# Reordering the opening of the expert layer in a two-layer decoder step

## The reference, cut to what matters

```python
scores = sigmoid(x @ w_router)                      # 264 x 64
biased = scores + router_bias
# 4 of 8 groups by the sum of their 2 best experts, then 8 of the experts left
idx    = top_k(where(group_open, biased, -inf), 8)
w      = scores[idx] / sum(scores[idx]) * 2.5
routed = sum over the 8 experts e of w[e] * (silu(x @ w_gate[e]) * (x @ w_up[e])) @ w_down[e]
shared = (silu(x @ ws_gate) * (x @ ws_up)) @ ws_down
f      = routed + shared
```

## Time and profile before

| what | us |
|---|---|
| runs, median of 3 (lowest, highest) | 1641.63 (1640.94, 1641.82) |
| span of the profiled execution | 1639.0 |
| TensorE busy in it | 1542.3 (94%) |
| VectorE / ScalarE / GpSimd busy | 734.1 / 372.5 / 96.3 |
| mean granted TensorE clock | 0.990 of full speed |
| first instruction of the opening, layer 0 (logits) | 369.33 |
| first product of round 0, layer 0 / layer 1 | 406.84 / 1122.11 |

### The profile page before, as it was taken

How to read it: one execution, slowest core, us unless ns; L and a number is a source line. 1 busy time by engine, 2 the same in 40 slices (tenths; PEclk the granted TensorE clock), 3 DMA queues, 4 the chain that set the end, 5 groups by cost and what they waited for, 6 DMA issues and landing times. The chain is left out here.

```text
span 1639.0 us, 29881 instructions
## 1 busy us (share of the span) xinstructions
PE 1542.3 (94%) x11300; PEld 1034.8 (63%) x11300; DVE 734.1 (45%) x2034; ACT 372.5 (23%) x784; POOL 96.3 (6%) x121
## 2 busy tenths in 40 slices
PE   6999989998999999999999899998999999999996
PEld 4778765776655655665565587766565566566553
DVE  3205435226464445345345335354745434533445
ACT  2002443113121121122111245332112112111122
POOL 0000100001000000000000001010000000000000
PEclk9999999999999999999999999999999999999998
DMA  9996799337999999999899783986999999998994
GB/s 366 386 371 245 291 397 388 110 129 323 376 420 420 420 420 420 419 419 418 344 390 416 245 267 122 375 320 259 419 420 421 420 420 421 418 418 342 378 420 187
DMA packets 150665, 580.21 MB, mean 354 GB/s; under 512 B 17341, under 2 KB 62561, under 8 KB 101290
## 3 DMA queue, kind: packets, MB, share of 16 engines
q1 hardware_dynamic: 134442, 535.74, 82.4%
q0 software_dynamic: 15488, 40.92, 6.5%
q10 hardware_dynamic: 640, 2.26, 0.3%
HBM read 568.22 MB, written 26.90 MB: 363 GB/s over the span
## 5 line engine op out<-in xcount | busy, mean ns | idle before, releaser
L2391 PE MATMUL ps<-ring,scratch 128*64 128x256 f32 x3840 | 428.5, 383 | 17.7 <-DMA ring<-in_moe_w_up 16.4
L2391 PEld LDWEIGHTS ps<-ring,scratch 128*64 128x64 f32 x3840 | 289.7, 138 | 143.6 <-issue 26.9
L2439 PE MATMUL ps<-ring,scratch 128*64 128x512 f32 x960 | 214.7, 597 | 0.2 <-DVE scratch L2837 0.2
L2352 PE MATMUL ps<-scratch 128*128 128x264 bf16 x1488 | 183.1, 277 | 5.2 <-issue 4.3
L2776 DVE SCALAR_TENSOR_TENSOR scratch<-scratch,ps 128x256 f32<-128x256 f32 x64 | 30.8, 481 | 348.5 <-ACT scratch L2929 341.6
L697 PE MATMUL ps<-hT,ring 128*128 128x264 f32 x768 | 180.5, 389 | 1.3 <-ACT hT L379 1.3
L2352 PEld LDWEIGHTS ps<-scratch 128*128 128x128 bf16 x1488 | 131.3, 97 | 57.8 <-issue 19.6
L697 PEld LDWEIGHTS ps<-hT,ring 128*128 128x128 f32 x768 | 146.0, 192 | 30.7 <-issue 2.5
L2439 PEld LDWEIGHTS ps<-ring,scratch 128*64 128x64 f32 x960 | 62.4, 136 | 126.2 <-issue 93.3
L2743 DVE TENSOR_TENSOR scratch<-scratch,ps 128x264 f32<-128x264 f32 x240 | 103.4, 431 | 76.7 <-PE ps L2352 76.4
L2929 ACT ACTIVATE scratch<-ps 128x256 f32<-128x256 f32 x64 | 24.6, 385 | 441.2 <-PE ps L2391 421.5
(11 more groups left out here) (403 smaller groups left out, 1376.2 us busy)
## 6 DMA issues: line engine op xcount, KB each, us to landing
ring<-in_moe_w_gate SPq DMA_DIRECT2D x128, 1024.0 KB, 17.6
ring<-in_moe_w_up SPq DMA_DIRECT2D x128, 1024.0 KB, 17.6
ring<-in_moe_w_down SPq DMA_DIRECT2D x128, 1024.0 KB, 18.2
ring<-in_ada_w SPq DMA_DIRECT2D x48, 1024.0 KB, 13.7
ring<-in_ret_w_in SPq DMA_DIRECT2D x24, 1024.0 KB, 16.9
ring<-in_state_ret SPq DMA_DIRECT2D x16, 1024.0 KB, 14.6
out_ret_sample<-ring POOLq DMA_DIRECT2D x16, 1024.0 KB, 9.1
ring<-in_gla_w_in SPq DMA_DIRECT2D x12, 1024.0 KB, 13.3
```

What stands on the lines that cost most here:

```text
L2352: mm = nc.tensor.matmul(k.ps[:, c % 2, 0:T], parts_of(p)[:, s, c * P:(c + 1) * P], slot_token[:, p, :], start=(p == 0 and s == 0), stop=(p ...
L2391: mm = nc.tensor.matmul(k.ps[lo:lo + CAP, 2 + p, j * DE:(j + 1) * DE], xg[:, p, c, lo:lo + CAP], slot(k, n, DE)[:, c, :], start=(c == 0), ...
L2439: mm = nc.tensor.matmul(k.ps[lo:lo + CAP, 6 + half, :], hid_t[:, p, m, lo:lo + CAP], slot(k, n, D)[:, m, half * 512:(half + 1) * 512], sta ...
```

## The change

Both expert layers are built by the same code, so the change holds twice. Its parts:

- TensorE transposes the scores ahead of token piece 0. Piece 1 gets PSUM banks 4 and 5 (`TOKEN_BANK`) and no longer waits; piece 2 waits for the copy of piece 0 and stands two chunks into the first half of the shared gate product. ScalarE copies and stores all three pieces before its first Silu.
- The ranks are placed 2 chunks into the second block of shared gate products, the row list of round 0 four chunks later.
- The gather of tile 0 stands ahead of the shared down product, the gather of tile 1 behind its first two chunks, then `slots_first`, then the other six chunks. The wait for both gathers' landing (`s_got`, 32) is therefore ahead of the shared down product.
- The row list of round 1 moves from ahead of round 0 to behind the gate and up products of its tile 0.
- VectorE turns the row list into indices ahead of the first two weight operations. `list_order` is split: its first part (`find_special`, to L2601) runs ahead of the shared hidden product, its second part after the copies of the gathered tiles.
- ScalarE copies its half of tile 0 ahead of the shared down chunks, its half of tile 1 behind the second chunk.

```diff
+    TOKEN_BANK = (6, 4, 6)
...
+        def gather_tile(pe, p, d):
+            for b in range(2):
+                if p:
+                    pe.wait_ge(g_odd if b else g_even, d + p)
+                for c in range(4):
+                    d0 = (4 * b + c) * P
+                    mm = nc.tensor.transpose(k.ps[:, b, c * P:(c + 1) * P], xtok_of(p)[:, d0:d0 + P], ident)
+                mm.then_inc(s_gat, 1)
...
+                if first and p == 0:
+                    list_rows(pe, 1)
...
+            if first:
+                pe.wait_ge(s_shx, DC)
             for p in range(min(tiles(r), PAIRS)):
                 hidden_first(pe, p, 6 + p, d)
...
+            def shared_down(chunks):
+                w = slot(k, n_sh + 2, D)
+                for c in chunks:
+                    if c >= 4:
+                        pe.wait_ge(s_shx, c - 3)
+                    for m in range(FC):
+                        mm = nc.tensor.matmul(k.ps[:, DOWN_BANK[c % 4], 0:T], w[:, m, c * P:(c + 1) * P], sh_hid[:, m],
+                                              start=(m == 0), stop=(m == FC - 1))
+                    mm.then_inc(s_shd if c < DC - 1 else k.ring_free[(n_sh + 2) % RING], 1)
...
-            token_major(0, *TOKENS[0])
             pe.wait_ge(s_frow, 1)
             cond_transpose(k, k.ps[:, 2], fill_rows).then_inc(s_fcrt, 1)
             pe.wait_ge(s_sig, 1)
...
-            token_major(1, *TOKENS[1])
+            token_major(0, *TOKENS[0], bank=TOKEN_BANK[0])
+            token_major(1, *TOKENS[1], bank=TOKEN_BANK[1])
             wait_slot(k, pe, n_sh)
             pe.wait_ge(s_fmod, 1)
-            shared(0, 0, range(DC)).then_inc(s_shg, 1)
-            token_major(2, *TOKENS[2])
-            shared(0, 1, range(DC)).then_inc(k.ring_free[n_sh % RING], 1)
+            shared(0, 0, range(2))
+            pe.wait_ge(s_natc, 1)
+            token_major(2, *TOKENS[2], bank=TOKEN_BANK[2])
+            shared(0, 0, range(2, DC)).then_inc(s_shg, 1)
+            shared(0, 1, range(2))
             pe.wait_ge(s_ch, 1)
...
+            shared(0, 1, range(2, 6))
+            pe.wait_ge(s_natc, TT)
+            list_rows(pe, 0, bank=6)
+            shared(0, 1, range(6, DC)).then_inc(k.ring_free[n_sh % RING], 1)
             wait_slot(k, pe, n_sh + 1)
             shared(1, 0, range(DC))
-            pe.wait_ge(s_natc, TT)
-            list_rows(pe, 0, bank=6)
             shared(1, 1, range(DC)).then_inc(k.ring_free[(n_sh + 1) % RING], 1)
+            pe.wait_ge(s_idxc, 1)
+            pe.wait_ge(s_got, 16 * PAIRS)
+            gather_tile(pe, 0, 0)
+            wait_slot(k, pe, n_sh + 2)
+            pe.wait_ge(s_shh, FC)
+            shared_down(range(2))
+            gather_tile(pe, 1, 0)
             pe.wait_ge(s_eye, 1 + 3 * (PAIRS + 1))
             pe.wait_ge(s_w0, 1)
-            pe.wait_ge(s_shh, FC)
             slots_first(pe)
-            ...
-            gather(pe, 0)
-            pe.wait_ge(s_shx, DC)
-            list_rows(pe, 1, bank=6)
+            shared_down(range(2, DC))
+            pe.wait_ge(s_shx, DC - 2)
             pe_round(pe, 0)
...
-            link(nc.vector.tensor_tensor(weight, score, chosen, ALU.mult))
-            link(nc.vector.tensor_reduce(total, weight, AX.X, ALU.add))
             v.wait_ge(s_idx, 1)
             row_numbers(PAIRS, bank=6, to=first_rows_at).then_inc(s_idxc, 1)
+            link(nc.vector.tensor_tensor(weight, score, chosen, ALU.mult))
+            link(nc.vector.tensor_reduce(total, weight, AX.X, ALU.add))
...
                 "p t (b e) s -> p b t (e s)", b=PAIRS)).then_inc(s_w0, 1)
+            find_special(v)
             wait_used(k, v, n_sh + 1)
...
+            take(v, 0, 0, nc.vector.tensor_copy, g_even)
             list_order(v)
             next_slots(1, [expert_at(v, EPI + e) for e in range(EPI)])
-            take(v, 0, 0, nc.vector.tensor_copy, g_even)
...
             token_rows_out(0, P)
             token_rows_out(1, P)
+            token_rows_out(2, NS)
             for m in range(FC):
...
-                if m == 0:
-                    token_rows_out(2, NS)
...
+            take_tile(act, 0, 1, nc.scalar.copy, g_odd, 0)
             for c in range(DC):
...
+                if c == 1:
+                    take_tile(act, 1, 1, nc.scalar.copy, g_odd, 0)
-            take(act, 0, 1, nc.scalar.copy, g_odd)
```

More of the change, by code:

```diff
@@ L2287, in gather @@
                 mm.then_inc(s_gat, 1)
+        def gather(pe, r, late=0):
+            d = done_tiles(r, late)
+            pe.wait_ge(s_got, 16 * (d + tiles(r)))
+            for p in range(tiles(r)):
+                gather_tile(pe, p, d)
         def spread_slots(pe, p):
@@ L2462, in _, with token_major @@
         def _(pe):
-            def token_major(t, n0, n):
-                if t:
-                    pe.wait_ge(s_natc, t)
+            def token_major(t, n0, n, bank):
                 for c in range(DC):
-                    mm = nc.tensor.transpose(k.ps[0:n, 6 + c // 4, (c % 4) * P:(c % 4 + 1) * P],
+                    mm = nc.tensor.transpose(k.ps[0:n, bank + c // 4, (c % 4) * P:(c % 4 + 1) * P],
                                              k.h[:, c, n0:n0 + n], ident)
@@ L2562, in weights_of, with take_tile @@
             return nc.vector.tensor_copy(to, w_parts[:, :, bass.ds(e, 1), :].rearrange("p t o s -> p t (o s)"))
+        def take_tile(eng, p, b, copy, sem, d):
+            eng.wait_ge(s_gat, 2 * d + 2 * p + b + 1)
+            copy(xg_of(p)[:, 4 * b:4 * b + 4, :].rearrange("p c n -> p (c n)"), k.ps[:, b, :]).then_inc(sem, 1)
         def take(eng, r, b, copy, sem, late=0):
             for p in range(tiles(r)):
-                eng.wait_ge(s_gat, 2 * done_tiles(r, late) + 2 * p + b + 1)
-                copy(xg_of(p)[:, 4 * b:4 * b + 4, :].rearrange("p c n -> p (c n)"), k.ps[:, b, :]).then_inc(sem, 1)
+                take_tile(eng, p, b, copy, sem, done_tiles(r, late))
         def last_of(kind, r, p):
@@ L2583, in rows_done, with find_special @@
                 eng.wait_ge(k.ring_free[n % RING], r + n // RING + 1)
-        def list_order(v):
+        def find_special(v):
             link = lambda ins: k.dve.link(v, ins)
@@ L2601, in list_order @@
             link(nc.vector.tensor_reduce(taken[0:1, 0:7], same, AX.X, ALU.add))
+        def list_order(v):
+            link = lambda ins: k.dve.link(v, ins)
             link(nc.vector.tensor_scalar(ordered[0:1, 0:7], taken[0:1, 0:7], -1.0, None, ALU.mult))
@@ L2851, in _ @@
             v.sem_inc(s_add, DC)
+            take(v, 0, 0, nc.vector.tensor_copy, g_even)
             list_order(v)
             next_slots(1, [expert_at(v, EPI + e) for e in range(EPI)])
[L2854 removed]
             v.wait_ge(s_idx, 2)
[L2856 removed]
+            row_numbers(PAIRS).then_inc(s_idxc, 1)
             round_(0)
@@ L2874, in token_rows_out @@
                 act.wait_ge(s_nat, t + 1)
+                bank = TOKEN_BANK[t]
                 nc.scalar.copy(token_rows[0:n, t, :].rearrange("p (k q) -> p k q", k=DC),
-                               k.ps[0:n, 6:8, :].rearrange("p b (q k) -> p k (b q)", k=DC)).then_inc(s_natc, 1)
+                               k.ps[0:n, bank:bank + 2, :].rearrange("p b (q k) -> p k (b q)", k=DC))\
+                    .then_inc(s_natc, 1)
                 act.wait_ge(s_natc, t + 1)
```

5 lines of the change are left out of this document (2 added, 3 removed).

## The result

| | median of 4 runs | lowest to highest | profiled execution: time, span |
|---|---|---|---|
| before | 1641.66 us | 1640.94 to 1641.82 | 1641.63, 1639.0 |
| after | 1651.01 us | 1649.75 to 1654.54 | 1654.54, 1652.7 |

What follows compares the result with a forecast made beforehand. The weight stream bounds the rounds, TensorE the opening. 1.7 + 2.3 + 0 + 2.4 = 6.4 us takes the span from 1639.0 to 1645.4, with 2.6 around it 1648.0 us; range for 8 in 10 1638.5 to 1652.0.

Steps and rivals of the forecast that it cites:

- part 7: Round 1's row list inside round 0: gathers in the full stream cost 1.2 us a layer; TensorE's wait taken as 0.
- Parts 1 to 3: Opening: row list 4.2 us earlier, stores' queue ends 0.86 later; stores decide, gathers go out within 0.3 us of before.
- Part 4: Opening, ahead of shared down: TensorE waits for both gathers' landing, 7.3 us in layer 0 and 7.9 in layer 1.
- Parts 5 and 6: Behind the wait: 9.5 us to round 0, which starts +1.7 and +2.3 us; TensorE's slow clock, no difference taken.
- The spare time: Round 1's down loads go out with some 4 us to spare, so the stream hides TensorE's wait for round 1's gathers.
- The third rival: Round 0: round 1's gather lands at 13.3 us, TensorE waits 6, stream hole, +2 in each layer, 1652 us; chance 0.13.
- The early landing: Opening: gathers there at about 394.5, wait at tile 0 below about 4 us, -5.2 in sum, 1636.4 us; chance 0.15.
- the halved wait: Opening: landing 5.7 us behind the issue saves 2.6 us in each layer, +1.2 in sum, 1642.8 us; chance 0.22.

Runs made afterwards that it cites:

- The experiment with the front alone: Kernel before with only scores ahead of token pieces, ranks and round 0's row list early, all behind as before: 1640.66 us, ratio 1.0001.
- The best version: Changed kernel with both gathers behind shared down, VectorE's tables ahead of tile copies, round 1's list ahead of round 0: 1633.50 us, 0.9952; again 1632.02 us, 0.9950.
- the neighbours: Two kernels compared with the best version: the same with round 1's list inside round 0 (1638.57 us), and the kernel before with the front alone (1640.66 us).
- a_again: Changed kernel, gathers still early, with round 1's row list, its tables and slots_first made ahead of the gather wait, second run: 1650.76 us, 1.0053.
- d_hold: Changed kernel with SyncE holding the last three down loads of round 0 until the first two gathers have landed: 1645.36 us, 1.0023.
- b_gather_late: Changed kernel with both gathers behind shared down, VectorE's tables ahead of its tile copies, round 1's list still inside round 0: 1638.57 us, 0.9984.
- e_two_queues: Changed kernel with the store of token piece 1 issued on GpSimd's own queue instead of ScalarE's: 1648.34 us, 1.0043.

## Why the prediction was right, and what it had wrong

The direction and the first wait were right; the sum was 3 us short of the median, and one term of it, in part 7, was sized wrong. That the time still lies in the wide range is partly luck: it is 1 us inside the end of the range, and the repeat of the changed kernel (1653.89) is outside.

**Parts 1 to 3** held. The index came 4.7 us earlier (forecast 4.2), the queue of the stores ended 0.6 and 0.8 us later (forecast 0.86), the gathers went out at the old time in layer 0 and 0.5 late in layer 1, and TensorE reached the gather at +22.4, as forecast. The experiment with the front alone shows that the earlier list buys nothing. That the stores alone decided already before was too strong: the index came last there (389.58 above), so the list was worth a few tenths until the stores moved back.

**Part 4** held: 7.75 and 7.95 us against 7.3 and 7.9. The gathers behind shared down, 0.69 and none, show that it is the order that exposes the landing; holding the loads shows what makes the landing long.

**Parts 5 and 6.** From the end of the wait to round 0 it takes 11.3 and 12.1 us, not 9.5. The granted clock is 0.69 over 401 to 408, below its full level for more than half of the time: the idle gap now lies ahead of the transposes and shared down, and they pay (1.94 instead of 1.03, 3.03 and 3.73 for a quarter of shared down that else takes 1.85). In return each tile of round 0 runs in 7.13 us, 14.3 for both instead of 15.62 and 16.37. Round 0 itself starts 3.9 and 5.0 us later than before, where 1.7 and 2.3 were forecast, and so that sign failed; but its tile 0, which frees the first slots, is 1.6 and 2.3 us shorter. So "no difference" was nearly right in sum: the stream restarts 2.4 and 2.7 us late, forecast 1.7 and 2.3. It was taken, not worked out, and that two misses cancel is luck. In layer 0, 0.5 us of that is a later landing.

**Part 7** is the step that failed, as a term of the sum. It had 1.2 us a layer for the gathers' own bytes, and for the stream behind TensorE's second wait it said "I take 0". Measured from the restart to the end of the stream are 2.3 and 3.4 us; in the other kernels with the list inside round 0, 2.7 to 4.2. The parts add up roughly: the hole of 1.4 and 2.1 us, and the gathers' 0.39 MB at 420 GB/s, 0.9 us, give 2.3 and 3.0. TensorE came for the gather 6.3 us behind its issue (422.38 to 428.71), about as forecast, but it landed at 10.0 instead of the 8.8 in the middle of the earlier trace rows: a wait of 3.64 and 3.91 us, inside the forecast's "0 to 6" but twice the 1.8 of its middle. The row was misread: the earlier trace rows mixes the first and the second gathers of the rounds, and TensorE waits for the second. In the kernel before, from round 2 on, the first ones took 7.8 to 9.0 us, 8.4 in the middle, and the second ones 9.7 to 11.2, 10.5 in the middle; the 13.3 is the third gather of the one round of the layer that has three. Round 2's second gather there (438.4 to 439):

```profile
scratch<-h_rows,scratch POOLq DMA_INDIRECT x1, 10.3
```

With 10.5 the forecast's own sum gives a wait of 3.5 us, near the one measured. The spare time failed with it. I counted "some 4 us" at the down loads of before; but the products of round 1 stand behind the second wait too, and the down loads went out 7.8 us later, 5.4 more than the restart. The third rival had this mechanism and priced it at 2 us in each layer over the forecast's 1.2; 1.1 and 2.2 were measured. It wanted a landing of 13.3 us for that, and 10 was enough, so 0.13 was too little.

**The early landing** (0.15) and **the halved wait** (0.22) didn't happen. The loads that are held show what the second would have needed.

**What was right in the change itself.** The removed idle pieces are real. The best version keeps them (round 0 starts 2.5 and 3.2 us earlier in the two layers of its first run, and its products take 14.03 us). What had to go back are the two moves that expose a landing, and with the gathers the order of VectorE's and ScalarE's tile copies. What pays, as far as the neighbours show, is the early `find_special`; the earlier list of round 0 and the token pieces, without it, gave 0.6 us, inside the interval.

**Open.** The start of the logits varied from 367.9 to 375.4 us among the profiled executions, with unchanged code ahead of it. It goes with TensorE's granted clock over 20 to 290 us: 0.99 in the seven executions whose logits start at 367.9 to 369.7, 0.98 in two at 370.4, 0.97 in four at 371.1 to 372.5, and 0.96 in the one at 375.4. The stretch in before and in that last one (`a_again`), clock in the third column from the end:

```profile
20.00:290.00 270.00, 256.40 (x1488) 188.40 (x1488) 98.22 (x213) 72.34 (x137) 14.51 (x20) 0.99 0.94 346
20.00:290.00 270.00, 255.54 (x1464) 188.03 (x1464) 93.97 (x204) 71.92 (x137) 14.18 (x20) 0.96 0.94 344
```

The whole times do the same: one run of before took 1636.74 us at a mean clock of 0.991, another 1644.47 at 0.986. The 1.8 us between the end of layer 0's stream and the end of the layer fall where the clock over 890 to 935 is 0.89 in after and 0.92 in before. So of the 13.7 us of the profiled span, the 2.0 ahead of layer 0 and these 1.8 go with the clock in code that is the same. Why it was lower is not shown; 0.96 and 0.97 came only in kernels with early gathers or the list inside round 0, but d_hold, b_gather_late and e_two_queues have these too and 0.98 or 0.99. In layer 0 of the kernel with early gathers and early list (2.4 to 4.6, and 2.1 to 3.3 in its second run) the loads' landings aren't in the trace, and where that part is lost stays open too.

## What to carry to other kernels

Before a consumer is moved ahead, look for when its transfer lands, not for when its index is ready; work that stands ahead of it may be the only cover. Small gathers belong in a gap of the stream: the same pair landed in 3.3 us there and in about 9 inside it. Where a stream sets the end, follow one number through the rounds, how late each round's load goes out against before: a flat line is the opening, a jump is a slot freed late. Then look where the same loads land, since only that shows how late the stream is. When TensorE waits for the second of two gathers, size the wait by the second ones alone.

## What the hardware showed that I hadn't expected

- Behind the issue of the first gather into the full stream, 3.9 us passed in layer 0 and 2.0 in layer 1 until the gathers' queue moved a packet; in the gap of the stream it was 1.6 us, and with the loads held 1.7. There the second gather landed 4.0 us behind its issue instead of 8.6.
- In the full stream the second gather of a round took 2 us longer than the first (in the kernel before, from round 2 on: 10.5 us in the middle of 26, against 8.4 in the middle of 28).
- Two microseconds of earlier issue moved the landing by 0.4 us in one layer and by 3.5 in the other.
- TensorE's clock was low behind the 7.75 us gap (0.69 over 7 us) and full again by round 0; in the better version, with no gap over 1.01 us in the opening, round 0 ran at the full clock.
